# GpSimd's tap products with a second operation: `mult` becomes `mult` followed by `add` of 0.0

## What is computed

```python
def causal_depthwise_conv(x, w, b):
    width = w.shape[0]
    y = lax.conv_general_dilated(
        x, w[:, None, :].astype(x.dtype), window_strides=(1,), padding=[(width - 1, 0)],
        dimension_numbers=('NWC', 'WIO', 'NWC'), feature_group_count=x.shape[-1])
    return y + b
...
    glu_a, glu_g = jnp.split(conv_in, 2, axis=-1)
    u = glu_a * jax.nn.sigmoid(glu_g)
    u = causal_depthwise_conv(u, conv_dw_w, conv_dw_b)
    u = jax.nn.silu(layer_norm(u, conv_ln_g, conv_ln_b))
    o_c = u @ w_conv_pw2 + b_conv_pw2
```

## Time and profile before

| what | us |
|---|---|
| three timed runs | 2844.94, 2846.03, 2844.15 |
| their median | 2844.94 |
| the profiled execution, its own time | 2844.26 |
| its span (first to last instruction) | 2842.4 |
| TensorE busy | 2770.7 (97%) |
| VectorE busy | 1662.5 (58%) |
| ScalarE busy | 1095.0 (39%) |
| GpSimd busy | 170.1 (6%), 132 instructions |

### The profile page before, as it was taken

How to read it: one execution, slowest core, us unless ns; L and a number is a source line. 1 busy time by engine, 2 the same in 40 slices (tenths; PEclk the granted TensorE clock), 3 DMA queues, 4 the chain that set the end, 5 groups by cost and what they waited for, 6 DMA issues and landing times.

```text
span 2842.4 us, 38582 instructions
## 1 busy us (share of the span) xinstructions
PE 2770.7 (97%) x15788; PEld 2291.8 (81%) x15788; DVE 1662.5 (58%) x2351; ACT 1095.0 (39%) x1656; POOL 170.1 (6%) x132
## 2 busy tenths in 40 slices
PE   8999999999999999999999999999999999999998
PEld 5778888997778889877878775888877788878998
DVE  4798447746995477555556425564664554364554
ACT  3545336544554266432223323222232222234443
POOL 0070000000520000000000000000000000000000
PEclk9999999999999999999999999999999999999999
DMA  8542457646523576455454212343435443221453
GB/s 338 198 155 80 139 181 238 223 164 221 171 82 112 176 254 227 159 180 183 148 193 156 89 56 78 141 157 126 148 119 185 179 154 141 97 97 45 163 185 113
DMA packets 121887, 444.12 MB, mean 156 GB/s; under 512 B 13424, under 2 KB 14832, under 8 KB 121328
## 3 DMA queue, kind: packets, MB, share of 16 engines
q1 hardware_dynamic: 121712, 441.66, 44.4%
HBM read 440.56 MB, written 1.05 MB: 155 GB/s over the span
## 4 chain that ended last, share of the span: by engine, by line
PE 87%; DVE 8%; ACT 3%; DMA 1%; issue 1%; SPq 0%; DVEq 0%; ACTq 0%
PE ps L621 23%; PE ps L622 22%; PE ps L623 22%; PE ps L625 19%; DVE rests L1660 2%; DVE area L1763 2%; DMA ring<-stream 1%; DVE rs L1723 1%; DVE area L1733 0%; DVE rt L1778 0%; ACT L1320 0%; ACT L1504 0%; DVE rt L1776 0%; ACT work L1320 0%; ACT L1274 0%
## 5 line engine op out<-in xcount | busy, mean ns | idle before, releaser
L621 PE MATMUL ps<-h_split,heads 128*128 128x256 f32 (+1 forms) x2960 | 980.5, 331 | 14.7 <-DVE h_split L1741 7.6
L622 PE MATMUL ps<-h_split,heads 128*128 128x256 f32 (+1 forms) x2960 | 957.9, 324 | 0.0
L623 PE MATMUL ps<-h_split,rests 128*128 128x256 f32 (+1 forms) x2960 | 957.7, 324 | 0.0
L1660 DVE TENSOR_TENSOR rests<-ring,heads 128x1024 fp32r<-128x1024 f32 x516 | 643.8, 1266 | 288.6 <-ACT heads L1260 280.9
L1260 ACT ACTIVATE heads<-ring 128x1024 fp32r<-128x1024 f32 x516 | 532.5, 1055 | 519.6 <-PE ps L623 300.9
L621 PEld LDWEIGHTS ps<-h_split,heads 128*128 128x128 f32 x2960 | 565.3, 191 | 119.0 <-ACT rt L1360 23.5
L622 PEld LDWEIGHTS ps<-h_split,heads 128*128 128x128 f32 x2960 | 565.5, 191 | 48.0 <-issue 5.3
L623 PEld LDWEIGHTS ps<-h_split,rests 128*128 128x128 f32 x2960 | 565.2, 191 | 44.1
L621 PE MATMUL ps<-hid_split,heads 128*128 128x256 f32 (+1 forms) x1056 | 355.1, 336 | 0.0
L623 PE MATMUL ps<-hid_split,rests 128*128 128x256 f32 (+1 forms) x1056 | 354.9, 336 | 0.0
L622 PE MATMUL ps<-hid_split,heads 128*128 128x256 f32 (+1 forms) x1056 | 354.8, 336 | 0.0
(11 more groups left out here) (184 smaller groups left out, 2481.5 us busy)
## 6 DMA issues: line engine op xcount, KB each, us to landing
ring<-stream SPq DMA_DIRECT2D x830, 512.0 KB, 3.8
consts<-constants SPq DMA_DIRECT2D x1, 1728.0 KB, 10.6
x_sb<-x_in SPq DMA_DIRECT2D x1, 1024.0 KB, 11.3
x_sb<-ctx_in SPq DMA_DIRECT2D x1, 1024.0 KB, 4.7
out<-area SPq DMA_DIRECT2D x1, 1024.0 KB, 4.8
consts<-constants SPq DMA_DIRECT2D x1, 576.0 KB, 10.3
cols<-columns SPq DMA_DIRECT2D x1, 538.0 KB, 10.1
cols<-columns SPq DMA_DIRECT2D x1, 157.5 KB, 2.2
```

The costliest lines, as they stand in the source:

```text
L621: nc.tensor.matmul(out, lhsT[0], rhs[0], start=first, stop=False)
L622: nc.tensor.matmul(out, lhsT[0], rhs[1], start=False, stop=False)
L623: ins = nc.tensor.matmul(out, lhsT[1], rhs[0], start=False, stop=last)
L1660: nc.vector.tensor_tensor(rests[:, u % RING, :], ring[:, u % RING, :], as_f32(heads[:, n % HEADS_RING, :]), ALU.subtract)\
```

## The change

`tensor_scalar` on GpSimd gets a second scalar and a second operation. Before, the instruction computed `u_pad * w`, with the second operation empty; after, it computes `u_pad * w + 0.0`. The weight is still read from `cols`, and the 0.0 is a constant in the instruction. The number of instructions, their tiles, their order, the waits and the semaphores stay as they are. VectorE's taps aren't touched.

```diff
@@ -1197,7 +1197,7 @@
                             pool.wait_ge(vector_done, V.at(("read", (p, "conv", c))))
                         w = col(f"conv_w_{l}", tap * CC + c)
                         nc.gpsimd.tensor_scalar(csq[:, c, :] if tap == 0 else product_[:, c, :], u_pad[:, c, tap:tap + SEQ],
-                                                w, None, ALU.mult)\
+                                                w, 0.0, ALU.mult, ALU.add)\
                           .then_inc(pool_done, G.mark())
                     pool.wait_ge(pool_done, G.n)
                     if tap > 0:
```

## The result

| kernel | median of its runs, us | ratio to before, 95% interval |
|---|---|---|
| before | 2844.7 (20 runs) | |
| after | 2847.8 (20 runs) | 1.0014 [1.0007, 1.002] |

The change makes the kernel 3 to 4 us slower, by a small but real amount. Runs of one kernel differ by some us with their mean granted clock (0.991 to 0.994 for the kernel before), and the loss is there at equal clock too: at 0.991 the runs of the kernel before that were made beside the experiments have a mean of 2845.1 us and those of the kernel after 2848.6, at 0.993 it is 2842.8 and 2846.3. The forecast was "no change" at 2844.9; the cheaper product, which is what came, was rival 1, at 2842 to 2848 us with a chance of 0.25.

The account below looks back on a forecast made before the run. TensorE was taken to bound the kernel, VectorE close behind; 64 products at about 0 us, hidden in slack, and unmoved sums added 0 to 2844.3 us profiled, so 2844.9 us against the runs, range 2831 to 2856 us.

Parts of the forecast that it names:

- rival 1: GpSimd's products get cheaper, 0.73 us or less, and GpSimd finishes 5 to 10 us sooner; 2842 to 2848 us, chance 0.25.
- The bound, the slack, nobody waits for the taps: TensorE binds, VectorE close behind; GpSimd's taps in the first two blocks end 59.0 and 59.4 us before VectorE adds them.
- The cost of one product: GpSimd's two-operation product on 128x256 was put at 0.90 us, give or take 0.15, the same as the old form.
- How the engines block each other: A two-input VectorE instruction waits out a whole GpSimd sum (2.23 us lost once); products hardly hold VectorE (0.19 us).
- the forecast's second term: GpSimd's seven sums in each of the first two blocks block VectorE where they did before; change 0 us.
- The stepping for a cheaper product: Queues stepped at 0.45 to 0.73 us a product: VectorE arrives at 205.2 to 207.1 us, -0.5 to +1.4 per block.
- What it is worth on the path: Per block, TensorE's waits of 4.7 and 1.7 us plus 2.5 us of slow clock, up to 8.9 us, depend on VectorE's arrival.
- rival 2: Products get dearer, 1.05 to 3.2 us, VectorE reaches the attention sooner, time falls 8 us to 2837; chance 0.17.

Follow-up runs that it names:

- e_forms: Against the kernel after: each of GpSimd's eight taps gets its own product form, with one or two operations, partly another result; 2838.8 us (one run).
- e_split: Against the kernel after: each GpSimd sum of 128x1024 is done as four of 128x256; 2837.5 us, ratio to before 0.9975.
- e_no_sums: Against the kernel after: the sums of taps 1 to 6 left out, so part of the computation is missing; 2829.8 us, ratio to before 0.9949.
- e_late: Against the kernel after: GpSimd starts its taps only when VectorE has scaled the attention's first maxima; 2865.8 us, ratio to before 1.0076.
- e_old_twice: Against the kernel before: old product form, each group of four products of taps 1 to 7 done twice; 2854.7 us, ratio to before 1.0034.
- e_first_old: Against the kernel after: products of taps 0 and 1 in the old one-operation form, taps 2 to 7 new; 2839.9 us, ratio to before 0.9987.

## Why the prediction was wrong, point by point

- **The bound, the slack, nobody waits for the taps:** right. The slack grew from 59 to 72 us and was worth nothing.
- **The cost of one product:** wrong, and this decided the forecast. I took 0.90 give or take 0.15 us, because the one-input product was dearer than the two-input sum and so looked like a general loop that passes both slots in any case. The product is 0.45 us, below the 0.735 us that I had as the nearest row. A loop that passes both slots in any case would give one price for one and for two operations; e_forms has 0.92 us for one, and 0.48 or about 1.14 us for two. The Trainium skill, "GPSIMD Engine Reference", section 3.1, has the rule that I had put aside because it didn't fit the old form: up to two operations run at 1.03 cycles an element. The new form agrees with it. GpSimd's sums of 256 and 1024 elements take 0.735 and 2.35 us, which leaves 0.20 us for an instruction without its elements; with that and the clock of 1.2 GHz from the same page of the Trainium skill, section 1, the rule gives 0.20 + 0.22 = 0.42 us, an estimate, against 0.45 measured. The other forms of e_forms, with one operation or two, don't agree with it (0.92 and about 1.14 us). The doubling that I took from section 7 of "GPSIMD Engine Reference" in the Trainium skill, 1.8 us, did not come.
- **How the engines block each other:** right in the main. A sum holds VectorE for what is left of it (L1779 took 2.81 us after, 0.85 before), a product hardly, and in pieces the same sum holds it less (e_split). "An instruction that reads two tensors" was too narrow: the one of 2.53 us at 202.66 is L1968, which reads one tensor and two columns, and it was held as well. For the products the rule of "SBUF — State Buffer" in the Trainium skill, on reading its port diagram, went on not to fit: 29 products of the new form held VectorE for 0.9 us in all (e_no_sums), 0.03 us each.
- **Where the sums fall:** the forecast's second term, "7 sums in each block fall where they fell", was put at 0 and measured 2.8 us in each block ahead of the attention. It failed with the price of the product. The stepping for a cheaper product was half right: "the same seven sums block VectorE, more of them early", up to 1.4 us a block later. What failed in it is that I stepped VectorE as if it never waited for anyone. I had the end of VectorE's first four tap instructions at 205.2 to 207.1 us; it came at 209.0. The sum at 166.4 came ahead of a rest that TensorE needed at once; TensorE ran dry, and VectorE got a wait that the trace before doesn't have, 3.7 us in the first block with the clock at 0.50 and 2.1 in the second at 1.00. Up to the add that makes 2.9 us in the first block and 1.6 in the second, 4.5 in all; the profiled spans differ by 3.7 and the medians by 3.1.
- **What it is worth on the path:** wrong in size, the other way. I let up to 8.9 us in a block depend on VectorE's arrival. e_late shows 2.4 us of earlier arrival for 9 us less blocking. And I priced a sum inside the attention at "up to 2.2" and took less; it is 1.5 to 2.5 on average, and with the one right behind the first maxima TensorE waits 3.2 us longer at a single place. From both followed the wrong sign of rival 2 (e_old_twice: +10 us, not -8).
- **The range:** it held the time, and partly by luck. It was wide enough for the forecast, the cheaper product and most of the dearer one. That the time moved so little is no merit of the sum: the product came out at half the price that the forecast had, and a gain of 3.7 us and a loss of 7.7 us partly cancelled. The chances gave the cheaper product 0.25 and slower by over 0.2% 0.18; it came out 0.14% slower, which the bound of 0.2% counts as the same.

So the change is a gain and a loss on top of each other. By the ratios, moving every sum but the first forward gives 3.7 us (e_first_old against before), and moving the first one as well takes 7.7 back (after against e_first_old).

## What to carry to other kernels

A faster instruction on a side engine isn't free of effects because the engine has slack: ask when its blocking instructions will now fall, and what the blocked engine is about to hand to the bound one. Cut long GpSimd instructions that read two tensors into short ones where VectorE works beside them; here that was worth 10 us against the whole sums, with the same products of the new form, and 5 us with those of the old form. When you step queues by hand, let every engine wait for the others, not only the two that you compare.

## What the hardware showed that I had not expected

- On GpSimd a `tensor_scalar` of 128x256 in float32 takes 0.45 us for multiply and add or multiply and multiply, 0.90 us for one operation alone, and at most 1.14 us for multiply and subtract and for add and add (multiply and maximum: 1.15).
- A gap of only 1.8 us on TensorE was followed by a granted clock of 0.50 in the window of 172 to 174 us, the same level as behind the gap of 4.7 us of the earlier trace rows. The length of the gap doesn't decide it: the same gap in the second block was followed by 1.00, and so was the one of 1.7 us in the first block of the kernel before, where the first line is the window with the gap:

```profile
186.00:188.00 2.00, 0.48 (x5) 0.28 (x3) 2.00 (x1) 1.40 (x2) 1.90 (x2) 1.00 0.17 39
188.00:190.00 2.00, 1.82 (x15) 1.82 (x16) 1.93 (x5) 0.94 (x1) 2.00 (x2) 1.00 0.58 223
```

What decides it stays open.
